# Residual input added by TensorE from one buffer, unit weights in idle buffers, and a ring of eight slots in every tile

## What is computed

```python
h = h + einsum('bsc,cd->bsd', mixed, w_out)
hf = rms_norm(h, norm_ffn_gain)
h = h + peer_ffn(hf, ...)
return rms_norm(h, norm_final_gain)
# peer_ffn, for each token:
q = einsum('td,dq->tq', h_t, w_query)          # 8 heads x 2 halves
s1, s2 = q1 . sub_keys_1, q2 . sub_keys_2      # 128 keys each
top 16 of s1 + s2  ->  experts (8 x 16 = 128), gates
act = gelu(h_t . expert_u[experts])
out = sum_k (gates * act)[k] * expert_v[experts[k]]
```

## Time and profile before

| | us |
|---|---|
| median of 3 runs | 3116.89 |
| lowest and highest | 3116.49, 3123.21 |
| profiled execution | 3123.21 |
| its span in the trace | 3121.4 |
| PE busy | 2303.5 (74%) |
| DVE busy | 2199.2 (70%) |
| ACT busy | 1506.3 (48%) |
| POOL busy | 1232.4 (39%) |
| DMA queue of the gathers, share of 16 engines | 84.1% |

### The profile page before, as it was taken

The page is one execution under the profiler, slowest core; times in us unless marked ns, Lnnn a source line. Parts: engine busy times, 40 slices in busy tenths (PEclk is TensorE's granted clock), DMA queues, the critical chain, the costliest instruction groups (busy, mean ns, idle before and its releaser), DMA issues.

```text
span 3121.4 us, 39271 instructions
## 1 busy us (share of the span) xinstructions
PE 2303.5 (74%) x13004; PEld 1081.1 (35%) x13004; DVE 2199.2 (70%) x5450; ACT 1506.3 (48%) x4168; POOL 1232.4 (39%) x1168
## 2 busy tenths in 40 slices
PE   8988687867787678866877677767786677765665
PEld 4447344423443244323433233323332233321211
DVE  1453687777777788778777777767777788776664
ACT  3433255655554455655554444544544444444443
POOL 1000343444444444443444444444444444444442
PEclk9999888988889888988899888988888889988777
DMA  3254599999999999999999999999999999999997
GB/s 121 78 188 142 227 384 376 405 411 389 406 387 411 418 403 372 401 414 408 385 389 411 399 413 394 402 421 398 409 400 412 399 416 414 402 408 421 421 421 329
DMA packets 192682, 1155.17 MB, mean 370 GB/s; under 512 B 20576, under 2 KB 48352, under 8 KB 60896
## 3 DMA queue, kind: packets, MB, share of 16 engines
q0 software_dynamic: 147456, 1073.81, 84.1%
q1 hardware_dynamic: 30560, 56.85, 5.2%
q10 hardware_dynamic: 14464, 22.02, 1.9%
HBM read 1136.61 MB, written 15.99 MB: 369 GB/s over the span
## 4 chain that ended last, share of the span: by engine, by line
DMA 37%; PE 29%; DVE 12%; ACT 7%; issue 4%; POOL 3%; POOLq 0%; ACTq 0%; DVEq 0%
DMA ring_mem<-in_experts,work 37%; PE bank L1503 15%; DVE ring_mem L1259 6%; PE bank L1451 3%; POOL ring_mem L721 3%; PE bank L1466 3%; PE bank L1291 3%; ACT work L956 1%; ACT work L952 1%; PE bank L1429 1%; PE bank L1385 1%; ACT work L950 1%; ACT L950 1%; ACT L863 1%; PE bank L1504 1%
## 5 line engine op out<-in xcount | busy, mean ns | idle before, releaser
L721 POOL DMA_INDIRECT ring_mem<-in_experts,work x1024 | 1160.7, 1134 | 1525.2 <-PE bank L1504 1330.4
L1259 DVE CUSTOM_DVE_ANT_0 ring_mem<-ring_mem,work 128x1024 f32<-128x1024 f32 x1024 | 1253.6, 1224 | 576.4 <-DMA ring_mem<-in_experts,work 566.7
L1503 PE MATMUL bank<-ring_mem,work 64*64 64x512 f32 x4096 | 1227.5, 726 | 552.6 <-ACT work L956 545.6
L1504 PE MATMUL bank<-ring_mem,work 64*64 64x512 f32 x4096 | 1227.7, 726 | 0.0
L950 ACT ACTIVATE work<-work 128x1 f32<-128x1 f32 x1024 | 206.5, 202 | 1204.7 <-DVE work L1259 1167.5
L1503 PEld LDWEIGHTS bank<-ring_mem,work 64*64 64x64 f32 x4096 | 294.1, 153 | 1212.2 <-ACT work L956 738.2
L956 ACT ACTIVATE work<-kept,work 128x64 f32<-128x64 f32 x1024 | 357.3, 349 | 33.5
L952 ACT ACTIVATE work<-work 128x1 f32<-128x1 f32 x1024 | 301.8, 295 | 33.3
L1291 PE MATMUL bank<-work 128*128 128x128 f32 x1080 | 195.0, 322 | 138.9 <-ACT work L818 73.9
L1504 PEld LDWEIGHTS bank<-ring_mem,work 64*64 64x64 f32 x4096 | 292.9, 153 | 0.0
L1291 PEld LDWEIGHTS bank<-work 128*128 128x128 f32 x1080 | 160.1, 219 | 275.8 <-ACT work L818 96.2
(11 more groups left out here) (269 smaller groups left out, 2234.0 us busy)
## 6 DMA issues: line engine op xcount, KB each, us to landing
ring_mem<-in_experts,work POOLq DMA_INDIRECT x1024
ring_mem<-in_wc ACTq DMA_DIRECT2D x31, 512.0 KB
ring_mem<-in_w_query SPq DMA_DIRECT2D x16, 576.0 KB, 4.1
late<-in_wc SPq DMA_DIRECT2D x16, 512.0 KB, 3.5
work<-kept_tiles SPq DMA_DIRECT2D x42, 128.0 KB
x_all<-in_w_out SPq DMA_DIRECT2D x1, 4096.0 KB, 13.8
work<-in_x SPq DMA_DIRECT2D x8, 512.0 KB
out<-work SPq DMA_DIRECT2D x8, 512.0 KB
```

The source lines that it names most:

```text
L721: G.indirect_dma_start(ring[slot(g)], None, a["experts"], bass.IndirectOffsetOnAxis(ap=pick_now[:, k:k + 1], axis=0)).then_inc(got[slot(g) ...
L1259: V.tensor_tensor_reduce(out=row, in0=row, in1=hf_tile[t % 2], scale=1.0, scalar=0.0, op0=ALU.mult, op1=ALU.add, accum_out=dots[:, k:k + 1 ...
L1503: PE.matmul(low_sum[half][high if odd else low], of[low], row[low], start=(q == 1), stop=(q == PICKS - 1))
L1504: m = PE.matmul(high_sum[half][low if odd else high], of[high], row[high], start=(q == 1), stop=(q == PICKS - 1))
```

## The change

- **One residual buffer.** `h_tile` becomes one buffer, `h_now`. x, the residual input, is added to the sums by TensorE: at pick 1 of each tile, ahead of its first pair, PE multiplies `h_now` with a 64-wide identity into the four accumulators, two products for each half. After this (`h_used`) the buffer is free. `take_sum` then works in `hf_tile`: it adds straight quarters to the crossed ones half by half, each after ACT's `crossed` of that half, and the last addition of 128x1024 is gone.
- **x is loaded later.** SP issues the load for tile t+1 at the end of its list of tile t, after the DeltaNet loads, when `h_now` is free again.
- **Weights of the units in idle buffers.** `w_now` is gone. In windows 1 to 4 the weights lie in `h_now`, in windows 5 to 7 and 0 in the place of four DeltaNet buffers (`idle_place`). Two of the 32 loads (units 5 and 21) move from k = 11 of the window before to k = 2 of their own; units 13 to 16 and 29 to 31 stood there before already.
- **Eight slots in all tiles.** With `w_now` out of the ring's memory and `EXTRA` larger by 1024 columns (`WORK` smaller by as many), the ring has eight slots from pick 0 on.

The diff, cut to its core:

```diff
-WORK = 9888
-EXTRA = 2086
+WORK = 9888 - 1024
+EXTRA = 3110
...
-        grow = Cut(ring_mem[:, EARLY_RING * 2 * DM:])
-        hn_now, w_now = grow(DB * PW), grow(DM)
+        grow = Cut(ring_mem[:, RING * 2 * DM:])
+        hn_now = grow(DB * PW)
...
-        spare = Cut(ring_mem[:, 3 * 2 * DM:EARLY_RING * 2 * DM])
+        spare = Cut(ring_mem[:, 4 * 2 * DM:RING * 2 * DM])
+        idle_place = work[:, lasting.at + cut.at:lasting.at + cut.at + DM]
...
+        def weights_place(w):
+            return h_now if 1 <= window(w) % PHEADS <= 4 else idle_place
+        def load_late(w):
+            return window(w) % PHEADS == 5 or (w - 1) % UNITS >= 12
... gpsimd
-                                if g == WIDEN:
-                                    pool.wait_ge(U["projected"], GROWN)
-                                pool.wait_ge(X["used"], USED0 + g + 1 - (EARLY_RING if g < WIDEN else RING))
+                                pool.wait_ge(X["used"], t * PICKS + j * TOPK + (USED0 + k - RING + 1))
... sync
                 def load_x(t):
-                    if t > 1:
-                        sp.wait_ge(X["out_made"], t - 1)
-                    sp.dma_start(h_tile[t % 2], ...)
+                    if t > 0:
+                        sp.wait_ge(X["h_used"], t)
+                        if t > 1:
+                            sp.wait_ge(X["f_sumsq"], t - 1)
+                        w = t * PHEADS - 4 - FIRST_WINDOW
+                        if 0 <= w < GROWN:
+                            sp.wait_ge(U["projected"], w + 1)
+                    sp.dma_start(h_now, ...)
... scalar
                     act.wait_ge(X["used"], t * PICKS + (USED0 + PICKS))
                     for half in range(2):
...
-                        m = A.activation(hf_tile[t % 2][high, cols], high_sum[half][low], ACT.Copy)
-                    m.then_inc(X["crossed"], 1)
+                        A.activation(hf_tile[t % 2][high, cols], high_sum[half][low], ACT.Copy).then_inc(X["crossed"], 1)
...
-                    A.activation(hf_tile[t % 2], h_tile[t % 2], ACT.Square, accum_out=f_stat[:, 0:1])
+                    act.wait_ge(X["straight"], t + 1)
+                    act.wait_ge(X["h_used"], min(t + 2, TILES))
+                    A.activation(h_now, hf_tile[t % 2], ACT.Square, accum_out=f_stat[:, 0:1])
...
+                        if j == 1:
+                            act.wait_ge(X["h_used"], tile + 1)
+                            if tile > 0:
+                                act.wait_ge(X["f_sumsq"], tile)
+                        if j == 5:
+                            act.wait_ge(D["gated_turned"], 2 * tile + 4)
+                            act.wait_ge(D["state_made"], nth(2 * tile + 3, 1, 2))
+                        act.dma_start(weights_place(w), a["wc"][...])
... vector, DeltaNet step 0
+                            w = (u // 2 - 1) * PHEADS - FIRST_WINDOW
+                            if u % 2 == 0 and 0 <= w < GROWN:
+                                dve.wait_ge(U["projected"], w + 1)
... vector
                 def take_sum(t):
-                    dve.wait_ge(X["used"], t * PICKS + (USED0 + PICKS))
-                    h = h_tile[t % 2]
+                    h = hf_tile[t % 2]
                     for half in range(2):
+                        dve.wait_ge(X["crossed"], 2 * t + half + 1)
                         V.tensor_tensor(h[low, cols], low_sum[half][low], h[low, cols], ALU.add)
                         m = V.tensor_tensor(h[high, cols], high_sum[half][high], h[high, cols], ALU.add)
                     m.then_inc(X["straight"], 1)
-                    dve.wait_ge(X["straight"], t + 1)
-                    dve.wait_ge(X["crossed"], t + 1)
-                    V.tensor_tensor(h, hf_tile[t % 2], h, ALU.add).then_inc(X["summed"], 1)
... tensor
+                        if q == 1:
+                            pe.wait_ge(X["h_made"], t + 1)
+                            for half in range(2):
+                                PE.matmul(low_sum[half][low], pair_ident[low], h_now[low, cols], start=True, stop=False)
+                                m = PE.matmul(high_sum[half][high], pair_ident[high], h_now[high, cols], start=True, stop=False)
+                            m.then_inc(X["h_used"], 1)
```

More of the change, by code:

```diff
@@ L37 @@
 RING = 8
-EARLY_RING = 7
 FRONT = 4
@@ L662, in deltas, with window @@
             return [(q - first, 2 * n + b) for b, first in enumerate(FIRST_SLOT) if 0 <= q - first < STEPS]
[L664 to L671, removed]
+        def window(w):
+            return w + FIRST_WINDOW
+        def weights_place(w):
+            return h_now if 1 <= window(w) % PHEADS <= 4 else idle_place
+        def load_late(w):
+            return window(w) % PHEADS == 5 or (w - 1) % UNITS >= 12
         def squares(units):
@@ L924, in unit @@
                         A.activation(raw_now[:, PAD:], bank[2][:, 0:PW], ACT.Copy).then_inc(U["raw_kept"], 1)
-                        if now < 12:
+                        if not load_late(w + 1):
                             load_unit(w + 1)
-                        else:
+                        if now >= 12:
                             act.wait_ge(U["second"], seconds(w))
@@ L1234, in unit @@
                         src = by_turns[(now - 12) % 2]
[L1235 removed]
+                        V.scalar_tensor_tensor(raw_now[:, PAD:], src[:, PAD:], 1.0 / taken, raw_now[:, PAD:], ALU.mult, ALU.subtract).then_inc(U["summed"], 1)
                 dve.wait_ge(gains_in, 16)
@@ L1278, in _ @@
                                 query(t + 1)
-                        unit(n, k)
+                        unit(n - FIRST_WINDOW, k)
                         if k == 11 and n + 1 < TILES * PHEADS:
@@ L1501, in _ @@
                                     of = diag[(k - 1 + odd) % DIAGS]
-                                    row = ring[slot(t * PICKS + q - 1 + odd)][:, DM + half * HALF:DM + (half + 1) * HALF]
-                                    PE.matmul(low_sum[half][high if odd else low], of[low], row[low], start=(q == 1), stop=(q == PICKS - 1))
-                                    m = PE.matmul(high_sum[half][low if odd else high], of[high], row[high], start=(q == 1), stop=(q == PICKS - 1))
+                                    row = ring[(k - 1 + odd) % RING][:, DM + half * HALF:DM + (half + 1) * HALF]
+                                    PE.matmul(low_sum[half][high if odd else low], of[low], row[low], start=(q == 1 and odd == 1), stop=(q == PICKS - 1))
+                                    m = PE.matmul(high_sum[half][low if odd else high], of[high], row[high], start=(q == 1 and odd == 1), stop=(q == PICKS - 1))
                                     if half == 1:
                                         m.then_inc(X["used"], 1)
-                        unit(t * PHEADS + j, k)
+                        unit(t * PHEADS + j - FIRST_WINDOW, k)
                         if t > 0 and q == FIN_GAIN:
```

63 lines of the change are left out of this document (31 added, 32 removed).

## The result

The changed kernel took 3068.6 us (median of 4 runs, 3067.5 to 3070.3) against 3119.0 for the kernel before (median of 4, 3116.5 to 3123.2): a ratio of 0.984 [0.983, 0.986], so 50 us or 1.6% faster. The profiled execution shown here took 3067.6 us.

The account below looks back on a forecast made before the run. The prediction took the gather queue, which runs dry when PE frees slots late, as the bound. Its terms, -23.9 - 0.5 + 2.0 = -22.4, taken as -22, gave 3095 us in median terms, range 3083 to 3113.

Parts of the forecast that it names:

- the sum: Whole kernel: -23.9 for the slot in tiles 0 to 3, -0.5 for tile 4, +2.0 for the residual, together -22.4 us.
- the two deep places: Around picks 22 and 54 of tiles 0 to 3: the eighth slot saves 2.49 us at each, 19.9 us in all.
- the lesser stalls: Rest of tiles 0 to 3: the slot saves 1.0 us a tile, 4.0 in all, bounds 0 and 2.4 a tile.
- rival 1: PE, DVE and ACT stay late after a stall, so the slot buys little: -2 to -6 us, 3113; chance 0.16.
- the term of the slot in tiles 0 to 3: Deep places 19.9 plus lesser stalls 4.0: 23.9 us saved, bounds 19.9 and 29.6.
- the first three windows of tile 4: Tile 4, where seven slots become eight: 0.5 us saved, range 0 to 2.5, one gather.
- The lower one: Lesser stalls gain nothing: outside windows 1 and 3, tile 2 loses 6.6 us, tile 5 with eight slots 7.8.
- The upper one: Lesser stalls gain 2.4 us a tile if the slot explains the whole difference of 18.1 - 10.75 between kinds of tile.
- Rival 3: Start of seven tiles: the residual lies on the path, 24 us against the slot's 10: +14, 3131; chance 0.06.
- Rival 4: Late loads of weights or x make PE wait 3 us in each of seven tiles: -1, 3116; chance 0.06.
- Rival 2: The slot buys the whole difference between kinds of tile, 29.6, and the residual warms PE's clock: 3084; chance 0.12.
- that sign: Tiles 5 to 7, with eight slots both times, becoming longer by 2 us or more would prove the forecast wrong (rival 3).

Follow-up runs that it names:

- the second trace of the changed kernel: The changed kernel run once more, unaltered, beside its variants: 3062.5 us, ratio 0.983 to the kernel before.

## Why the prediction was wrong in size and right in kind

**What held.** The gain comes from the eighth slot; the other edits give -3 us (-9 to +2.5) where the sum had +2.0. POOL's waits for PE fell by 38 us ("some tens"), and the two deep places stayed and became shallower.

**The deep places gave less than their term.** In the two places that the prediction shows (pick 22 of tile 2, pick 54 of tile 1) the queue lost 3.2 and 4.8 us and now loses 1.4 and 1.7. That is 4.9 less, where I had 2 x 2.49 = 5.0; but it is 1.8 and 3.1, not 2.49 each, so the agreement of the sum is luck. Over four tiles the deepest 8 us of windows 1 and 3 gave 3.8 a tile, 15.3 in all and not 19.9, and one of them, in tile 0, still loses 3.1, more than the 1 to 2.5 forecast.

**The step that failed: the lesser stalls.** The sum gave them 1.0 us a tile (bounds 0 and 2.4). The slot gave 9.9 us a tile over all traces (11.3 in the pair of the table), of which the deep places are 3.8, so the rest gave 6.1 to 7.5. By the means of the table above, windows 1 and 3 became 6.4 us shorter, 2.6 more than their deep places explain, and the six other windows some 5.0. The largest of these is window 0 with 2.1: the prediction had read a stall of 2.9 us at the start of tile 5 (rival 1) and gave it no term. So the term of the slot in tiles 0 to 3 was 19.9 + 4.0 where it is some 40. A second term was too small in the same way: the first three windows of tile 4, 0.5 us (at most 2.5), where the traces have 338.8 - 332.9 = 5.9. Together that is 45, and the runs have 46 for the slot. Both bounds of the lesser stalls were wrong:

- *The lower one*, which I took to be near, compared tile 2 outside windows 1 and 3 with tile 5 (6.6 against 7.8 us lost). It holds two kinds of tile and one execution of each. Tiles without units do gain from the slot: with seven slots about tile 5 takes 343.0 us at 398 GB/s, and the eight-slot executions have 329 to 339. Rival 1's evidence, window 1 of tile 4 against tile 5, misled in the same way: over a whole tile a slot is worth some 8 us there.
- *The upper one* let the slot bring tiles 0 to 3 to the 10.75 us lost in tiles 5 and 6. They now lose 6.7 on average, less than those did. Two things speak against the comparison. The 10.75 was one execution's figure: tiles 5 and 6 of the changed kernel lose 3.1 and 12.0. And the lost time isn't independent of the bytes: without the weights' 38.6 us of transfers the kernel gained 22.8 us only, and tile 2 with seven slots lost 3.8 us more. So the bytes of the units can fill gaps of the queue that a tile without them leaves empty.

**Under it lay a wrong picture of the chain.** I argued against rival 1 that PE and DVE have a quarter of each tile free, and took each stall as one that stands alone. That quarter is a mean over the tile. Windows 1 and 3 take 43 to 44.5 us with eight slots, with half the bytes and with the weights left out: here the engines are the slower ones, against 41.1 us of the queue, and they catch up in the other windows. In the deepest places it is PE that is busy all the time. Slots are then a store of time that is drawn down over a whole window, and not only a cushion for one stall of a few us. That each slot less costs more than the one before it fits this: 344, 354 and 384 us a tile with eight, seven and six (means of traces; the last from one execution, 19 us above its kernel's median).

The store is argued, not shown. Another picture fits as well: each slot is taken for a whole round, from the issue of its gather through DVE, ACT and PE, and with too few slots that round sets the pace everywhere. With six slots all eight windows of a tile are longer, by 3.1 to 8.3 us against the changed kernel, not windows 1 and 3 alone. No run separates the two, nor how much of the 43 us each engine's waits make up; that stays open.

**The residual on PE.** PE, ACT and DVE at the start of tile 5 in the changed kernel (for the earlier trace rows):

```profile
2063.55 0.59 ACT L875 ACTIVATE work<-bank 64x512 f32<-64x512 f32 x1 [2.67 <-PE bank L1525]
...
2064.78 0.68 DVE L1188 TENSOR_TENSOR work<-bank,work 64x512 f32<-64x512 f32 x1 [2.04 <-ACT work L876]
...
2067.61 1.23 DVE L1273 CUSTOM_DVE_ANT_0 ring_mem<-ring_mem,work 128x1024 f32<-128x1024 f32 x1
...
2067.64 0.92 PE L1515 MATMUL bank<-work,kept 64*64 64x512 f32 x1 [4.17 <-DVE work L1189]
...
2069.86 1.11 PE L1524 MATMUL bank<-ring_mem,work 64*64 64x512 f32 x1
...
2070.05 1.06 PE L1515 MATMUL bank<-work,kept 64*64 64x512 f32 x1
```

PE starts on the residual 4.1 us after ACT's start, when the quarters are read (I had 4.0), and DVE is at the dot product of pick 1 then, as before: right. The first pair starts at 2069.86, 6.4 us after the last one's end at 2063.45, as before. I had it held back by 1.1 us at half clock, behind the residual. It was not: the last residual products (2070.05) and the first of the pair (2069.86) run beside each other. The window from the pair's start:

```profile
2069.90:2072.50 2.60, 2.60 (x20) 0.99 (x16) 2.60 (x8) 1.35 (x5) 0.00 (x0) 0.73 1.02 425
```

The granted clock is 0.73 here, where it was 0.50 in the first pair before. Four of the 20 records are the residual's last; the pair's own 16 run from 2069.86 to 2072.98, 3.1 us, and before the change from 2122.19 to 2125.88, 3.7 us. So the gain that I had bounded at 1.7 us a tile is there in this tile with 0.6, and the loss isn't. That would be -4 us in seven tiles if all of it lay on the path; the run with this edit alone had -5 [-10, 0] by its ratio, which can't tell it from nothing. Rival 3 is out: nothing was slower.

**x and the weights.** What the changed kernel's page lists of these loads (KB, median us to landing), for the earlier trace rows:

```profile
ring_mem<-in_experts,work POOLq DMA_INDIRECT x1024, 12.4
work<-in_wc ACTq DMA_DIRECT2D x31, 512.0 KB, 8.3
...
work<-in_x SPq DMA_DIRECT2D x8, 512.0 KB, 9.5
```

The load of x in tile 1 is issued at 900.8 us and wanted at 927.2. Whom its reader L1100 waits for, in the changed kernel (us, times):

```profile
  PE bank L1465: 45.5, 8
```

It waits for PE's projection alone, and never for x; and PE's products of the units (L1443) list no wait for a load either. Rival 4 is out, as the run with x loaded late said too (0.9995).

**The rivals.** Rival 1 (3113) expected tiles 0 to 3 to keep 355 us: they have 343 to 346, and the prediction's own 349 to 351 was too long as well. Its doubt about a chain that stays late was sound, but the slot gave more for it, not less. Rival 2 (3084) was nearest, and for a reason that is half right: the whole difference between the kinds of tile and more. The prediction said that it would be wrong if tiles 5 to 7 became longer by 2 us or more. Tile 7 did, by 2.2 (1.5 by the starts of its dot products), but in the second trace of the changed kernel it is 1.5 us shorter than before: executions with the same slots differ by as much, so that sign was badly chosen.

## What to carry to other kernels

A slot of a gather ring can't be priced by the one or two deepest stalls of a trace. Look for windows in which the engines are slower than the queue: halve the bytes of the transfers and leave all instructions, and check a window so found against a run that takes bytes away elsewhere, since a window can hold work put off in the one before. Here each slot less cost more than the last. Read a stall in every tile in which it occurs, not in the one where it is deepest. Before taking a stretch with more slots as the bound of what a slot can buy, ask whether its load on the queue is the same, and look at a second execution. And a share of 0.98 of the DMA engines doesn't mean that only bytes count: here the last hundredths of it were worth 50 us.

## What the runs showed of the hardware

- Bytes beside a gather queue that has gaps are partly free: 38.6 us worth of weight loads cost 22.8 us with eight slots and about 19.6 with seven (the two can't be told apart).
- With nine slots about tile 4 runs at 419 GB/s over 329 us, nearly the 421 of an undisturbed window. So the rate of one window is very nearly held for a whole tile. The Trainium skill, "DMA: Bandwidth & Descriptors", section "Where 436 GB/s comes from", has about 358 GB/s as what binds from HBM to SBUF. The runs, on one core, show more again. The page's own section "Measured (HBM→SBUF, 128 partitions, SWDGE, issued from GpSimd)" has 425 GB/s for a core alone and takes about 358 for both cores of a pair at work, which no run here shows; the 419 to 421 of these runs are near the 425.
- Where the queue ran driest in windows 1 and 3 of tiles 0 to 3 of the kernel before, PE was busy throughout, 8.00 of 8 us. It isn't so everywhere: at the start of tile 5 the queue fell to 119 GB/s with PE busy for 2.22 of 4 us.
- Products of 64x64 quarters of two different loops, the residual's and the pair's, were in flight together, at 1.06 and 1.11 us each.
